# Expert gate and up weights loaded as consecutive rows per partition, tokens gathered by every eighth column

## The reference, cut to what matters

```
t = rmsnorm(x, ln2_g)                                  # 256 x 1024
logits of groups and experts = t @ w_router_*          # contraction over 1024
combine[n, e]: weight of the two chosen experts of a token, else 0
for e in range(16):
    a = silu(t @ w_gate[e]) * (t @ w_up[e])            # w_gate, w_up: 1024 x 512
    y = y + combine[:, e:e+1] * (a @ w_down[e])        # w_down: 512 x 1024
```

## Time and profile before

| what | value |
|---|---|
| median of 3 runs | 1318.02 us (1315.42 to 1320.92) |
| profiled execution | 1321.09 us, span 1319.1 us |
| mean granted TensorE clock | 0.897 of full speed |
| TensorE busy | 1130.6 us (86%) |
| VectorE busy | 751.9 us (57%) |
| ScalarE busy | 613.4 us (47%) |
| weight loads of gate and up | 32 + 32 of 1024 KB each |

### The profile page before, as it was taken

The page is one execution under the profiler, slowest core; times in us unless marked ns, Lnnn a source line. Parts: engine busy times, 40 slices in busy tenths (PEclk is TensorE's granted clock), DMA queues, the critical chain, the costliest instruction groups (busy, mean ns, idle before and its releaser), DMA issues.

```text
span 1319.1 us, 13972 instructions
## 1 busy us (share of the span) xinstructions
PE 1130.6 (86%) x5373; PEld 932.2 (71%) x5373; DVE 751.9 (57%) x845; ACT 613.4 (47%) x708; POOL 33.7 (3%) x44
## 2 busy tenths in 40 slices
PE   5965978786768999999995999996898888999997
PEld 4754855675657777777774788885778776788886
DVE  4413322956466787787787555554455653555553
ACT  5423354003327777877875444442462433433341
POOL 0000011510000000000000000000000000000000
PEclk9987975568858999999998999998886979999999
DMA  8658601003316988988984555574224001555520
GB/s 288 187 83 290 201 33 64 0 16 118 95 64 228 339 318 312 344 314 315 345 314 169 191 191 189 187 248 142 97 81 174 1 1 64 163 189 190 191 95 32
DMA packets 118468, 226.34 MB, mean 172 GB/s; under 512 B 6118, under 2 KB 14541, under 8 KB 118414
## 3 DMA queue, kind: packets, MB, share of 16 engines
q1 hardware_dynamic: 117730, 224.14, 50.9%
q0 software_dynamic: 368, 1.21, 0.3%
q10 hardware_dynamic: 316, 0.24, 0.1%
HBM read 221.39 MB, written 4.19 MB: 171 GB/s over the span
## 4 chain that ended last, share of the span: by engine, by line
PE 70%; DVE 15%; ACT 7%; issue 4%; another core or an unknown queue 2%; ACTq 1%; DMA 0%; POOL 0%; DVEq 0%
PE ps L1445 15%; PE ps L1446 15%; PE ps L1447 15%; DVE w_lo L811 6%; PE ps L1686 4%; ACT w_hi L495 4%; PE ps L1687 4%; PE ps L1899 2%; PE ps L1712 2%; PE ps L1732 1%; PE ps L1855 1%; DVE h_lo L838 1%; DVE arena L943 1%; DVE y_lo L1180 1%
## 5 line engine op out<-in xcount | busy, mean ns | idle before, releaser
L811 DVE TENSOR_TENSOR w_lo<-w_raw,w_hi 128x2048 fp32r<-128x2048 f32 x204 | 465.3, 2288 | 287.8 <-ACT w_hi L495 287.6
L495 ACT ACTIVATE w_hi<-w_raw 128x2048 fp32r<-128x2048 f32 x204 | 388.5, 1913 | 331.5 <-PE ps L1447 259.8
L1445 PE MATMUL ps<-w_hi,h_hi 128*128 128x512 f32 (+1 forms) x720 | 281.0, 390 | 49.9 <-DVE w_lo L811 27.7
L1446 PE MATMUL ps<-w_lo,h_hi 128*128 128x512 f32 (+1 forms) x720 | 278.2, 386 | 0.0
L1447 PE MATMUL ps<-w_hi,h_lo 128*128 128x512 f32 (+1 forms) x720 | 278.0, 386 | 0.0
L1445 PEld LDWEIGHTS ps<-w_hi,h_hi 128*128 128x128 f32 x720 | 138.8, 193 | 79.3 <-issue 28.7
L1447 PEld LDWEIGHTS ps<-w_hi,h_lo 128*128 128x128 f32 x720 | 138.3, 192 | 26.9
L1446 PEld LDWEIGHTS ps<-w_lo,h_hi 128*128 128x128 f32 x720 | 138.8, 193 | 26.0
L1445 PE MATMUL ps<-w_hi,aT_hi 128*128 128x512 f32 x176 | 69.8, 396 | 7.7 <-DVE aT_lo L1092 6.0
L1447 PE MATMUL ps<-w_hi,aT_lo 128*128 128x512 f32 x176 | 69.5, 395 | 0.0
L1446 PE MATMUL ps<-w_lo,aT_hi 128*128 128x512 f32 x176 | 69.5, 395 | 0.0
(11 more groups left out here) (318 smaller groups left out, 1442.2 us busy)
## 6 DMA issues: line engine op xcount, KB each, us to landing
w_raw<-in_ffn_w_in SPq DMA_DIRECT2D x44, 1024.0 KB, 5.2
w_raw<-in_w_exp_gate SPq DMA_DIRECT2D x32, 1024.0 KB, 5.4
w_raw<-in_w_exp_up SPq DMA_DIRECT2D x32, 1024.0 KB, 6.4
w_raw<-in_w_exp_down SPq DMA_DIRECT2D x32, 1024.0 KB, 7.4
w_raw<-in_w_in SPq DMA_DIRECT2D x22, 1024.0 KB, 11.5
w_raw<-in_ffn_w_out SPq DMA_DIRECT2D x22, 1024.0 KB, 5.0
w_raw<-in_w_mix_in SPq DMA_DIRECT2D x8, 1024.0 KB, 5.3
w_raw<-in_w_out SPq DMA_DIRECT2D x4, 1024.0 KB, 5.0
```

Source lines behind the costliest of these rows:

```text
L495: act.activation(w_hi[:, u % SPLIT, :], w_raw[:, u % RAW, :], ACT.Copy).then_inc(hi_ready, 1)
L811: dve.tensor_tensor(w_lo[:, u % SPLIT, :], w_raw[:, u % RAW, :], w_hi[:, u % SPLIT, :], ALU.subtract).then_inc(lo_ready, 1)
L1445: pe.matmul(out, hi, w_h, start=first, stop=False)
L1446: pe.matmul(out, hi, w_l, start=False, stop=False)
```

## The change

The rows of w_gate and w_up are dealt to the partitions in another way. Before, partition p held rows p, 128 + p, 256 + p and so on, one for each of the 8 tiles. Now partition p holds the 8 consecutive rows 8p to 8p + 7, and tile k is the set of rows k, 8 + k, 16 + k and so on. A unit is 4 of the 8 rows, so per partition it was 4 pieces of 2 KB in memory and is one piece of 8 KB. The router's weights are dealt alike. The token side has to match: tile k of the tokens is every eighth column from column k on, in the gather and in the transposes before the router. w_down and all other weights are as before.

```diff
         def moe_src(e, j):
             if j < 4:
                 w = a["w_exp_gate"] if j < 2 else a["w_exp_up"]
-                v = w[0].rearrange("e (k p) n -> e p k n", p=P)
+                v = w[0].rearrange("e (p k) n -> e p k n", k=KT)
...
-                        sp.dma_start(wr_raw[:, :, 0:4], a["w_router_group"][0].rearrange("(k p) n -> p k n", p=P)).then_inc(wr_in, 16)
-                        sp.dma_start(wr_raw[:, :, 4:20], a["w_router_expert"][0].rearrange("(k p) n -> p k n", p=P)).then_inc(wr_in, 16)
+                        sp.dma_start(wr_raw[:, :, 0:4], a["w_router_group"][0].rearrange("(p k) n -> p k n", k=KT)).then_inc(wr_in, 16)
+                        sp.dma_start(wr_raw[:, :, 4:20], a["w_router_expert"][0].rearrange("(p k) n -> p k n", k=KT)).then_inc(wr_in, 16)
...
-                            ins = pe.transpose(ps[:, b, c0:c0 + P], src[:, tt, k * P:(k + 1) * P], ident)
+                            cols_of = slice(k, D, KT) if t == 2 else slice(k * P, (k + 1) * P)
+                            ins = pe.transpose(ps[:, b, c0:c0 + P], src[:, tt, cols_of], ident)
...
                 pair = pick[:, :, 2 * (n // 4):2 * (n // 4) + 2, 0:SLOTS]
                 for k in range(2):
                     o = ps[:, chunk_bank(n), 256 * k:256 * k + 256].rearrange("p (e l s) -> p l e s", e=2, l=2)
-                    c = slice((2 * (n % 4) + k) * P, (2 * (n % 4) + k + 1) * P)
+                    c = slice(2 * (n % 4) + k, D, KT)
                     for part, h2 in enumerate((h2_hi, h2_lo)):
                         for tt in range(TT):
                             ins = pe.matmul(o[:, part], h2[:, tt, c], pair[:, tt], start=(tt == 0), stop=(tt == 1))
```

## The result

| what | before | after |
|---|---|---|
| median of 8 runs each | 1317.14 us (1315.16 to 1320.92) | 1330.99 us (1324.13 to 1336.15) |
| ratio of the times | | 1.0103, 95% interval 1.0075 to 1.0131 |
| profiled execution, span | 1321.09 us, 1319.1 us | 1335.14 us, 1333.1 us |
| mean granted TensorE clock | 0.897 | 0.893 |
| DMA packets | 118468 | 93892 |

The change makes the kernel slower by 1.0%. The forecast was 1318 us, no change. The runs of the changed kernel are further apart than those of before, and by and large those with the higher mean clock are the shorter: 1324.13 us at 0.906, 1329.96 us at 0.896, 1336.15 us at 0.889.

What follows compares the result with a forecast made beforehand. The prediction took the experts' stage to go at TensorE's pace with ScalarE and VectorE in the loop, loads hidden. Its terms summed 0 + 0 + 0 + 0, so 1318 us; range 1312 to 1339, likeliest 1314 to 1323.

Steps and rivals of the forecast that it cites:

- What bounds the kernel: Experts' stage: goes at the pace of TensorE with ScalarE and VectorE; loads hidden with at least 2 us to spare.
- the loads: 64 expert weight loads, one 8 KB piece per partition: valued at 0, with 3 us either way for the range.
- The second rival: Experts' stage: cheaper loads make the whole stage a little quicker, at most 3% of 266 us, 1310 us; chance 0.07.
- the third: Expert loads: the change does not reach the transfers, which stay in 2 KB packets; 1318 us; chance 0.04.
- The strided stationary operand in the gathers: 256 gather products reading stationary columns with a step of 8 numbers: the deciding term, valued at 0.
- the upper bound of 0.62 us: Gathers: at most 4.9 ns per stepped column, a product going from 0.112 to 0.62 us, some +93 us in all.
- The first rival: Gathers: strided weight load takes twice as long and leaves the slack; 1327 to 1339 us, middle 1331; chance 0.34.
- Per expert: First rival's sum for both gather calls after hidden waits: 0.7 us per expert, +9 us over 13 experts.
- The penalty at the low clock: First rival: 40 gather products and 16 transposes add 12 us if the penalty is in cycles of the throttled clock.
- The slack: Waits behind both gather calls: a product may cost half as much again, 0.44 us per call, before the expert lengthens.
- The signs named beforehand: Gather spacing: 0.112 us confirms the forecast; 0.22 us means waits for y_lo gone and expert about 20.2 us.
- The signs for the loads: Expert loads: fewer or larger DMA packets, landing at or below 6.3 us, still no wait on them.

Runs made afterwards that it cites:

- experiment 1: Changed kernel with contiguous columns on the token side, so only the loads differ from the kernel before: 1318.52 us, ratio 0.999 to the kernel before.
- Experiment 10: Kernel before, moving operand of the gathers read at steps 1 to 32 by call, from the fifth call on: 1320.92 us, one run.
- experiment 8: Kernel before, stationary operand of the gathers read at steps 1 to 16 by call, from the fifth call on: 1328.79 us, one run.
- experiment 7: Kernel before, every eighth column only in each expert's second gather call, from call number 5 on: 1317.14 us, ratio 0.9997.
- experiment 6: Kernel before, every eighth column only in each expert's first gather call, from call number 4 on: 1332.3 us, ratio 1.0127.
- Experiment 5: Kernel before, each gather call from the fifth on issuing 18 contiguous products in place of 8, some repeated: 1326.39 us, ratio 1.0068.
- experiments 2: Kernel before, only the gather's column slice changed to every eighth column, loads and transposes as before: 1335.0 us, ratio 1.0095.
- experiment 9: Kernel before, all gathers as plain fp32 products, even calls contiguous and odd calls stepped: 1353.36 us, one run.

## Why the prediction was wrong

**What bounds the kernel, and the loads.** Right. No wait ends with a load of experts in either kernel, and the loads alone are worth nothing (experiment 1). The second rival, a quicker stage from lighter loads, falls with it; the third falls by the packet count.

**The strided stationary operand in the gathers: the step that failed.** The prediction wrote "The ends are far apart; I take the value of the nearest row, 0". That row, L1855, had its step on the moving operand. Experiment 10 shows that this side pays nothing up to a step of 32, experiment 8 that the stationary side pays double from a step of 4. So the row said nothing on the question, and no row of before did. The prediction had itself just found that the stationary load is what a gather pays for. With that, a row about the other operand could not lower the chance of a penalty, and the upper bound of 0.62 us, taken from the same row, bounded nothing either. The rule of the Trainium skill in "SBUF — State Buffer", under the port swizzle, spoke against the change, and of its direction the trace agrees: 0.240 us in place of 0.112. Its limit agrees only in part: by it a step of 4 is still free, while experiment 8 measures 0.233 us there.

**The first rival was the right mechanism.** It took a factor of two, 0.224 us per product, and came to 1327 to 1339 us with 1331 in the middle; measured are 0.240 us and 1330.99 us. Inside it, several sizes were off:

- *Per expert* it said 0.7 us, measured is 0.50. It let both calls share the loss. In fact the second call is hidden entirely (experiment 7) and the first alone costs the 0.5 (experiment 6). It took ScalarE's copy ahead of the next expert for a fixed point 0.1 us away, but that copy moves with the first call.
- *The penalty at the low clock.* It allowed 12 us for 56 operations if the penalty were in throttled cycles. It is a fixed time: 0.240 us per product at either level, so at 1.2 GHz only 0.027 us more than the 0.214 of before, 0.85 us for the 32. The router's 16 transposes take 3.28 us before and after.
- *The drops of the clock* were not foreseen. Three stretches of 3.4 us cost 1.5 us each, 4.5 us of the 14. Experiment 5 ties them to calls of stepped loads. They appeared where the first call, which follows directly on products with few columns, was stepped (experiments 2 and 6, the changed kernel; once in experiment 8, at 562.9 us behind a first call with step 5), and not where only the second was (experiment 7). Plain fp32 products stepped in the second call gave none either. Why they come in some experts and not in each is open.

The total therefore came near 1331 partly by luck: 0.2 us per expert too much and up to 12 us of throttled cycles that are not there stood against the 4.5 us of low clock.

**The slack.** The prediction held that a product may cost half as much again before the expert grows. That was right: with 0.173 us per product in the first call and 0.233 in the second the expert stays at 19.53 us (experiment 8). For the second call even the double is free (experiment 7).

**What would show it.** The signs named beforehand came out on the side of the rival: a spacing above 0.17 us, the waits for y_lo gone, an expert at 20.0 us (20.2 was said). The signs for the loads held too: fewer packets, landing as before and no wait on an expert load.

## What to carry to other kernels

A stride is priced by the operand that carries it and by the engine that reads it: look for a row with the step on the same operand, and if there is none, call the price unknown instead of 0. When both sides of a contraction can be permuted, leave the stationary operand contiguous and let a transpose, a moving operand or a copy made once absorb the step. Before making a load's pieces larger, look whether anything waits for that load.

## What the hardware showed that was not expected

- A product with 128 stationary fp32 or fp32r columns costs 0.112 us at 2.4 GHz and 0.214 us at 1.2 GHz with contiguous columns, but 0.240 us at both levels with a step of 8: the stepped read does not follow TensorE's clock.
- For TensorE's stationary operand, steps of 4 to 16 numbers cost the same within 0.02 us (0.221 to 0.240), a step of 2 almost nothing (0.117), a step of 3 half (0.173).
- Transposes by TensorE with the same stepped stationary operand take 0.116 us at full clock (0.108 contiguous) and 0.205 us at 1.2 GHz (the same contiguous). What spares them is open; the type is not it (experiment 9).
- ScalarE and VectorE read 128x2048 fp32 with a step of 32 bytes in 4.01 and 3.96 us, contiguous in 1.91 and 2.28 us.
- Pieces of 8 KB in place of 2 KB leave the landing of a 1 MB load (w_gate and w_up) at 5.3 and 6.6 us, where it was 5.4 and 6.4 (5.4 and 6.8 in experiment 1).
- Eight steps of the moving operand, up to 32 numbers, cost 0.110 to 0.120 us per product, and the contiguous one 0.112.
